# Seams of the expert layer: queries on half the tokens, finer waits, the last value blocks tile by tile

## The reference

```python
hp = layer_norm(ALPHA * hp + mix_p, ln1_g[l], ln1_b[l])
...
q = (tok @ w_q).astype(jnp.float32).reshape(n, PEER_HEADS, 2, PEER_DKEY // 2)
s1 = jnp.einsum('nhk,ek->nhe', q[:, :, 0], sk[0])
s2 = jnp.einsum('nhk,ek->nhe', q[:, :, 1], sk[1])
v1, i1 = lax.top_k(s1, PEER_TOPK)
v2, i2 = lax.top_k(s2, PEER_TOPK)
...
gate = jax.nn.softmax(top_s, axis=-1).astype(h.dtype)
...
act = jax.nn.gelu(jnp.einsum('nd,nhkd->nhk', t, u_tab[e]), approximate=False)
return jnp.einsum('nhk,nhkd->nd', g * act, v_tab[e])
...
hp = layer_norm(ALPHA * hp + peer_ffn(hp, *pw), ln2_g[l], ln2_b[l])
```

## Time and profile before

| | us |
|---|---|
| median of 3 runs | 2153.55 (2152.06 to 2166.17) |
| the profiled execution, its own time | 2161.72 |
| its span, first to last instruction | 2159.3 |
| TensorE busy | 2044.9 (95%) |
| VectorE busy | 1485.2 (69%) |
| moved by DMA | 682.97 MB, mean 316 GB/s |

### The profile page before, as it was taken

One profiled execution on the slowest core, in us unless ns is written; L12 is line 12 of the kernel. 1 busy time (PEld: TensorE's weight loads), 2 busy tenths in 40 slices (PEclk: granted clock), 3 DMA queues, 4 the chain that ended last, 5 costly groups with the idle time before them and its releaser, 6 DMA issues.

```text
span 2159.3 us, 33707 instructions
## 1 busy us (share of the span) xinstructions
PE 2044.9 (95%) x12186; PEld 1709.8 (79%) x12186; DVE 1485.2 (69%) x3108; ACT 742.2 (34%) x1111; POOL 787.3 (36%) x485
## 2 busy tenths in 40 slices
PE   7999999998978997999999999999979999999996
PEld 7999985555542346989999999999978888778784
DVE  1375125664662333678888879999789888988888
ACT  2232113443440001224333355555433333333332
POOL 4343210000210003336898841221365564656440
PEclk9999998999988998999999999999999999999998
DMA  9999987883968668936999977888999999999992
GB/s 325 346 315 311 318 324 292 341 354 139 339 235 318 235 221 323 347 116 223 352 361 357 340 284 274 306 299 302 359 388 390 389 393 393 389 385 391 387 387 104
DMA packets 202346, 682.97 MB, mean 316 GB/s; under 512 B 18305, under 2 KB 84225, under 8 KB 194177
## 3 DMA queue, kind: packets, MB, share of 16 engines
q1 hardware_dynamic: 150832, 439.29, 56.4%
q0 software_dynamic: 46080, 167.79, 20.3%
q10 hardware_dynamic: 5328, 74.52, 9.9%
HBM read 618.78 MB, written 196.32 MB: 377 GB/s over the span
## 4 chain that ended last, share of the span: by engine, by line
PE 58%; DMA 19%; DVE 9%; issue 9%; POOL 3%; ACT 2%; SPq 0%; POOLq 0%; DVEq 0%; ACTq 0%
DMA overlay<-peer_v 15%; PE bank L188 12%; PE bank L189 12%; PE bank L190 12%; PE bank L1426 5%; PE bank L2014 4%; POOL overlay L358 3%; DVE overlay L2212 3%; DVE arena L2027 2%; PE bank L644 2%; PE bank L628 2%; DMA arena<-cache_v 1%; ACT overlay L2131 1%; PE bank L694 1%; PE bank L667 1%
## 5 line engine op out<-in xcount | busy, mean ns | idle before, releaser
L188 PE MATMUL bank<-overlay 128*128 128x384 f32 (+4 forms) x2832 | 959.7, 339 | 46.5 <-DVE overlay L2216 17.0
L189 PE MATMUL bank<-overlay 128*128 128x384 f32 (+4 forms) x2832 | 946.2, 334 | 0.0
L190 PE MATMUL bank<-overlay 128*128 128x384 f32 (+4 forms) x2832 | 945.2, 334 | 0.0
L188 PEld LDWEIGHTS bank<-overlay 128*128 128x128 f32 (+1 forms) x2832 | 535.4, 189 | 87.0 <-issue 39.1
L189 PEld LDWEIGHTS bank<-overlay 128*128 128x128 f32 (+1 forms) x2832 | 535.3, 189 | 30.3
L190 PEld LDWEIGHTS bank<-overlay 128*128 128x128 f32 (+1 forms) x2832 | 534.5, 189 | 31.2
L1850 POOL DMA_INDIRECT arena<-peer_v,arena x160 | 267.4, 1671 | 228.0 <-DVE arena L2027 205.1
L1578 POOL TENSOR_TENSOR overlay<-overlay 128x1024 fp32r<-128x1024 f32 x86 | 206.5, 2404 | 316.0 <-ACT overlay L1571 312.9
L2027 DVE SCALAR_TENSOR_TENSOR arena<-arena 128x1024 f32<-128x1024 f32 x160 | 204.3, 1277 | 0.1
L1850 POOL DMA_INDIRECT arena<-peer_rows,arena x80 | 106.6, 1332 | 245.8 <-DVE arena L2022 225.0
L1571 ACT CAST overlay<-overlay 128x1024 fp32r<-128x1024 f32 x144 | 150.0, 1044 | 114.7 <-DMA overlay<-peer_u 90.6
(11 more groups left out here) (235 smaller groups left out, 2160.9 us busy)
## 6 DMA issues: line engine op xcount, KB each, us to landing
overlay<-peer_u SPq DMA_DIRECT2D x128, 512.0 KB, 7.6
overlay<-peer_v SPq DMA_DIRECT2D x128, 512.0 KB, 11.3
o_ks<-cache_k ACTq DMA_DIRECT2D x11, 4088.0 KB, 18.4
o_vsall<-cache_vall SPq DMA_DIRECT2D x21, 2044.0 KB, 23.5
arena<-cache_kT SPq DMA_DIRECT2D x32, 896.0 KB, 11.2
arena<-cache_v SPq DMA_DIRECT2D x56, 512.0 KB, 6.9
arena<-w_out SPq DMA_DIRECT2D x48, 512.0 KB, 5.6
act<-arena SPq DMA_DIRECT2D x128, 192.0 KB, 8.2
```

The lines of the kernel that those rows point to most:

```text
L188: pe.matmul(out, lhs[0], rhs[0], start=start, stop=False)
L189: pe.matmul(out, lhs[0], rhs[1], start=False, stop=False)
L190: return pe.matmul(out, lhs[1], rhs[0], start=False, stop=stop)
```

## The change

1. **Queries.** The first half of features 0 and 1 (24 matmuls each) is issued around the last `turn_h`: TensorE waits only for the splits of the first three tiles. ScalarE casts the first weights before and behind the last norm's root, GpSimd makes the first low part before that norm's end and the others behind it. The three DMAs L1541 move behind the queries.
2. **Up.** The copy into banks 4 and 5 moves behind the fourth Gelu; TensorE no longer waits for VectorE's copies of the scores.
3. **Value stage, start.** SyncE waits for two stores of each slot before the first group and for all behind it; ScalarE doesn't wait for the stores; VectorE waits for one slot's stores at each of blocks 2 to 5. One accumulator is cleared before the waits, the other behind block 0.
4. **Value stage, end.** Late rows are spread over 120 blocks; the norms of tile 3 and the sample tokens stand behind blocks 121 and 123; gain and bias of the norm are fetched ahead of the last group; the last four blocks are multiplied tile by tile, and each tile's norm waits for its own.

```diff
@@ pe_out
+            pe.wait_ge(h_lo, 2 * 3)
+            query_half(pe, 0, 0)
             turn_h(pe, 4)
+            query_half(pe, 1, 0)
@@ act_out
+                if i == 3:
+                    act.wait_ge(mixed, TILES)
+                    hi_of(act, 0, 0)
+                    hi_of(act, 1, 0)
                 act_root(act, n, i)
+                if i == 3:
+                    hi_of(act, 2, 0)
+                    hi_of(act, 3, 0)
...
-            for g in range(1, FOLD):
-                act.dma_start(h1[g * NS:(g + 1) * NS, QT], h1[0:NS, QT]).then_inc(h_folded, 16)
@@ pool_query
+            lo(0, 0)
+            pool.wait_ge(ln_step.sem, lnm["out", QT])
+            for s in range(1, 4):
+                lo(s, s)
@@ pe_query
+        def query_half(pe, f, half):
+            pe.wait_ge(u_lo, f + 1)
+            for c in range(DC):
+                mm = product(pe, bank[:, 2 * (f % 2) + half, 0:HALF], [w[:, f % 4, c] for w in us],
+                             [h[:, c, half * HALF:(half + 1) * HALF] for h in hh], c == 0, c == DC - 1)
+            return mm
...
+            def query(f):
+                if f >= 2:
+                    pe.wait_ge(q_kept, f + 1)
+                    query_half(pe, f, 0)
+                query_half(pe, f, 1).then_inc(q_ready, 1)
@@ act_query
-            act.wait_ge(mixed, TILES)
-            for s in range(4):
-                hi_of(act, s, 0)
...
+            for g in range(1, FOLD):
+                act.dma_start(h1[g * NS:(g + 1) * NS, QT], h1[0:NS, QT]).then_inc(h_folded, 16)
@@ act_up
-            act.wait_ge(s_ready, QF + 2)
-            act.wait_ge(s_kept, 2 * QF + 4)
-            act.copy(bank[:, 4:6, :], h1[:, DT].rearrange("p (b n) -> p b n", b=2)).then_inc(h_copied, 1)
...
+                if n == 3:
+                    act.wait_ge(s_kept, 2 * QF + 4)
+                    act.copy(bank[:, 4:6, :], h1[:, DT].rearrange("p (b n) -> p b n", b=2)).then_inc(h_copied, 1)
@@ pe_up
-            pe.wait_ge(s_kept, 2 * QF + 4)
@@ values
-        ROWS_END, FINAL_AT = PK - 4, (PK - 3, PK - 1)
+        ROWS_END, FINAL_AT, BY_TILE = PK - 8, (PK - 7, PK - 5), 4
@@ sp_values
-                sp.wait_ge(a_stored[s], 16 * (GROUPS + 1))
+                sp.wait_ge(a_stored[s], 16 * (1 + 2))
...
             group(0, 1)
-            with sp.Fori(1, PAIRS) as x:
+            for s in range(4):
+                sp.wait_ge(a_stored[s], 16 * (GROUPS + 1))
+            with sp.Fori(1, PAIRS - 1) as x:
...
+            group(PAIRS - 1, 0)
+            sp_norm2(sp)
+            group(PAIRS - 1, 1)
@@ act_values
-            for s in range(4):
-                act.wait_ge(a_stored[s], 16 * (GROUPS + 1))
...
-                    if last and j == 6:
-                        act_root(act, TILES, LAST[0])
+                    if last and j in (2, 4):
+                        act_root(act, TILES + j // 2 - 1, LAST[j // 2 - 1])
@@ pe_values
+                for j in range(8 - BY_TILE if last else 8):
+                    ready(j)
...
+                if last:
+                    for i in range(DT):
+                        for j in range(8 - BY_TILE, 8):
+                            if i == 0:
+                                ready(j)
+                            mm = tile(j, i)
+                        mm.then_inc(tile_done, 1)
@@ dve_values
+            dve.memset(acc3, 0.0).then_inc(acc_zeroed, 1)
             dve.wait_ge(u_done, PK)
             dve.wait_ge(g_done, SLABS * GS + 2)
-            for s in range(4):
-                dve.wait_ge(a_stored[s], 16 * (GROUPS + 1))
-            dve.memset(acc3, 0.0).then_inc(acc_zeroed, 1)
-            dve.memset(accS, 0.0).then_inc(acc_zeroed, 1)
...
+                if 2 <= a < 6:
+                    dve.wait_ge(a_stored[a - 2], 16 * (GROUPS + 1))
                 dve.tensor_tensor(ga[1][:, j], prod[j % 2], ga[0][:, j].bitcast(F32), ALU.subtract).then_inc(ga_lo, 1)
+                if a == 0:
+                    dve.memset(accS, 0.0).then_inc(acc_zeroed, 1)
@@ final_norm
-                    dve.wait_ge(vp_done, PK + 8)
+                    dve.wait_ge(tile_done, i + 1)
```

More of the change, by code:

```diff
@@ L1578, in lo @@
                 pool.tensor_tensor(us[1][:, s], uraw[s], us[0][:, s].bitcast(F32), ALU.subtract).then_inc(u_lo, 1)
-            with pool.Fori(0, (QF + ROWS_FROM) // 4) as x:
+            lo(0, 0)
+            pool.wait_ge(ln_step.sem, lnm["out", QT])
+            for s in range(1, 4):
+                lo(s, s)
+            with pool.Fori(1, (QF + ROWS_FROM) // 4) as x:
                 for s in range(4):
@@ L1604, in pe_query @@
             pe.sem_inc(s_ready, 2)
-            def query(f, s):
-                pe.wait_ge(u_lo, f + 1)
-                pe.wait_ge(q_kept, f + 1)
-                for half in range(2):
-                    for c in range(DC):
-                        mm = product(pe, bank[:, 2 * (s % 2) + half, 0:HALF], [w[:, s, c] for w in us],
-                                     [h[:, c, half * HALF:(half + 1) * HALF] for h in hh], c == 0, c == DC - 1)
-                mm.then_inc(q_ready, 1)
+            def query(f):
[3 more added lines that the diff above has]
+                query_half(pe, f, 1).then_inc(q_ready, 1)
             def score(f, s):
@@ L1625, in pe_query @@
                     if s < 4:
-                        query(k * 4 + s, s)
+                        query(k * 4 + s)
                     if s:
@@ L2152, in pair, with ready, tile @@
             def pair(x, first=False, last=False):
-                for j in range(8):
+                def ready(j):
                     pe.wait_ge(ga_lo, x * 8 + (j + 3))
                     pe.wait_ge(v_lo, x * 8 + (j + 5))
+                def tile(j, i):
+                    for half in range(2):
+                        mm = product(pe, bank[:, 2 * i + half, :], [w[:, j, i * P:(i + 1) * P] for w in ga],
+                                     [v[:, j, half * 512:(half + 1) * 512] for v in vs], first and j == 0, last and j == 7)
+                    return mm
+                for j in range(8 - BY_TILE if last else 8):
+                    ready(j)
                     for i in range(DT):
-                        for half in range(2):
-                            mm = product(pe, bank[:, 2 * i + half, :], [w[:, j, i * P:(i + 1) * P] for w in ga],
-                                         [v[:, j, half * 512:(half + 1) * 512] for v in vs], first and j == 0, last and j == 7)
+                        mm = tile(j, i)
                     mm.then_inc(vp_done, 1)
-                    if last and j == 4:
+                    if last and j == 1:
                         unfold(pe)
+                if last:
[3 more added lines that the diff above has]
+                                ready(j)
+                            mm = tile(j, i)
+                        mm.then_inc(tile_done, 1)
             pair(0, first=True)
@@ L2235, in sp_final @@
             sp.dma_start(lnb2, t["ln2_b"]).then_inc(ln2_in, 16)
+        def sp_final(sp):
             for n, i in enumerate(LAST):
@@ L2276, in act_final @@
         def act_final(act):
-            for n in range(1, TILES):
+            for n in range(2, TILES):
                 act_root(act, TILES + n, LAST[n])
```

4 lines of the change are left out of this document (2 added, 2 removed).

## The result

| | before | changed |
|---|---|---|
| median, first comparison (us) | 2157.64 (4 runs) | 2132.55 (4 runs) |
| ratio, with its 95% interval | | 0.989 (0.9862 to 0.9918) |
| median, second comparison (us) | 2155.47 (15 runs) | 2137.3 (10 runs) |
| ratio, with its 95% interval | | 0.993 (0.9907 to 0.9953) |
| profiled execution | 2161.72 | 2126.72 |

The change makes the kernel 25.1 us faster in the first comparison and 18.2 in the second. Forecast were 2131.5 us and a gain of 21.9.

The account below looks back on a forecast made before the run. TensorE was taken to bound the kernel upstream, TensorE and the DMA within 3% in the value stage; -11.2-6.1-4.6 = -21.9 from the 2153.55 median gave 2131.5 us (own range 2126 to 2137, full range 2118 to 2145).

Parts of the forecast that it names:

- rival B: Tail and pace: packed rows cost their full 7.5 us and an upstream gain is smaller; -15.0, 2138.5 us; chance 0.23.
- Part 1, forecast -11.2: Queries: first half features start around the last norm, second query's copy at 838.3, not 849.6; bounds 9.3 to 11.2.
- it fell near 826, and a restart at 824.7 comes before that: Queries: TensorE restarts before its granted clock falls, so no slow clock; otherwise it costs about 1.9 us.
- a first query at half clock: Queries: sign that the prediction is wrong, the first query running at TensorE's slow clock.
- Covered by 4 us: Queries: the fifth query's weights are ready at 849.4, and TensorE asks for them at about 853.
- Part 2, forecast -6.1: Before the up stage: wait shrinks by 4.3 us and the slow start, costed at 1.8, vanishes; bounds 5.2 to 7.1.
- the issues begin with the start of the operation before them and take 2.81: Before the up stage: three DMA issues on ScalarE's queue delay its signals to 957.3, leaving TensorE about 1 us idle.
- Part 3, forecast -0.7: Value stage start: TensorE starts 7.3 us earlier, but the DMA limit returns all but 0.7 as waits; bounds 0 and 7.3.
- Rival A: Value stage: supply is not the limit, so the 7.3 us arrive and the tail gives more; -33.6, 2120 us; chance 0.22.
- Part 4, forecast -3.9: Value stage end: packed rows cost 2.5 us, last matmul ends 6.4 later, but one norm follows instead of three.
- VectorE's two norms now stand ahead of four splits: Value stage end: the reason given for TensorE's last matmul ending 6.4 us later than before, at 2146.2.
- Rival C: From the queries on: DMA engines are the limit, upstream gains return as waits; +4.4, 2158 us; chance 0.05.

Follow-up runs that it names:

- the single parts: The kernel before with the lines of one part of the change each, four kernels; ratios 0.9968, 0.9962, 1.0001 and 1.0006.
- in the pair: One profile of the kernel before against one of the changed kernel; profiled executions 2161.72 and 2126.72 us.
- part 2 alone: The kernel before with only the copy into banks 4 and 5 moved behind the fourth Gelu; 2149.16 us, ratio 0.9962.
- in company: The changed kernel with waits and clearings at the head of the value stage as before; 2137.32 us against 2137.3, ratio 0.9916.
- fewer bytes: The kernel before with gates of eight of twelve slabs unread, plus the finer waits at the value stage's start; executed once, 2132.87 us.
- The kernel with the late norm: The changed kernel with the sample tokens' norm behind block 127, not 123; 2135.52 us, ratio 0.9905 to the kernel before.
- fewer gates: The kernel before with the gates of eight of the twelve slabs left unread in the value stage; executed once, 2156.57 us.

## Why the prediction was right

The time (2131.5, measured 2132.55 and 2137.3), the gain (21.9, measured 25.1 and 18.2; by stretches 22.8 and 19.8) and the mechanism held. Part of the near hit is luck: against the single parts (10.1, 8.1, 0.9 and 2.2, together 21.3) two terms were 1.1 and 1.7 too large and one 2.0 too small. The second comparison's 2137.3 lies 0.3 above the forecast's own range and 1.2 below rival B's time, so the time alone doesn't choose between them; the terms do. Term by term:

**Part 1, forecast -11.2, measured -10.1.** The first query matmul came 3.72 us behind tile 3 (forecast about 3.7) and the copy 18.5 behind it. The prediction's last paragraph gives 28.5 for that copy, which is the length before; its own working says 838.3-821.1 = 17.2. What failed is one step: "it fell near 826, and a restart at 824.7 comes before that". That read a time of falling out of one seam. Here the clock fell with the restart, after 3.72 us of idleness (in three of the seven profiles ahead of it, in four behind), and the first 15 matmuls took 0.225 us each from start to start ((816.45-813.08)/15), not 0.126, which is 1.5 us; the text's lower bound, 9.3, had costed 1.9. The rule of the Trainium skill ("TensorE: Matmul & The Clock Gate", What's actually happening), by which the clock comes back only after sustained work, fits the windows of 813 to 816, and "a first query at half clock", named as a sign of rival B, came true. B's second half, rows at their full 7.5 us, did not: they cost 3.6. "Covered by 4 us" was too sure as well: in two of seven profiles 3.2 and 3.6 us went back to late weights.

**Part 2, forecast -6.1, measured -7.2 in the pair, -8.1 alone.** The upper bound (7.1, "if they blocked nothing") was the true one. The step that failed is "the issues begin with the start of the operation before them and take 2.81": they began 0.4 us ahead of the last cast and took 0.62+1.44 = 2.1, so they were over 0.4 us before TensorE ended its last score and not 0.8 behind it. With part 2 alone no issue stands there, and the wait is gone just the same. The selections of VectorE cost nothing, as costed.

**Part 3, forecast -0.7, measured -0.9 alone, 0 to -3 in company.** The step that decided the case held: a seam of 7.2 us was taken away and the stage took it back. With fewer bytes the same edit gave 8.5, so it is the supply that took it back; that the supply's limit is the DMA rate and not the latency of its loop rests on the estimate above (401 GB/s needed, 391 moved). Rival A (2120, "the supply is not the limit") falls with it.

**Part 4, forecast -3.9, measured -2.2 alone.** The size was near, the reason only half right. Packing the rows delayed block 120's split by 3.6 us (forecast 2.5) and its first matmul by 7.1. The last matmul came 40.1 behind the split, forecast 39.7; but by my text because "VectorE's two norms now stand ahead of four splits", and by the runs because TensorE is 3.5 us behind the split when block 120 comes (with no rows left VectorE makes the last splits faster than TensorE multiplies: at blocks 118 to 120 TensorE is 1.9, 2.7 and 3.5 us behind them) and then works through 34.9 us of its own and 1.7 that the second norm costs. The kernel with the late norm showed that: 7.3 us sooner on VectorE made this stretch 1.7 shorter, not the 5.3 by which the forecast's 39.7 exceeds TensorE's own 34.4. Block 127 came 27.5 us behind block 120, as forecast, by luck: gain and bias, which had 2 us in that sum, were no term: issued at 2071.48, waited for by nobody at 2078.14. The wait that did stand there, 1.90 us for the unfolding, I hadn't seen; it filled their place. The last paragraph's "last matmul 10 us, not 17, before VectorE's last operation" is a slip too: the sum has one norm there, 5.5, and 5.7 was measured.

**Rival C** (the queries at the DMA limit too) lives only in those 3 us of late weights; part 2 kept its 8.1 us to the end. The prediction let C hold by the 358 GB/s of the Trainium skill ("DMA: Bandwidth & Descriptors", Where 436 GB/s comes from). That doesn't follow: the up stage before moved 313 GB/s on average and 292 to 298 in 1200 to 1500, which is below the figure. And the 387 to 389 GB/s of the value stage contradict it again.

What stays open: why TensorE's clock stands at 1.2 GHz for 55 us upstream of tile 3 in one execution and for 85 in another, and the 3.3 us of wander of "120 ready", which bounds what can be said of parts 3 and 4 apart.

## What to carry to other kernels

Before you cost a wait at its length, look whether the engine behind it is held by its supply later in the stage. A high DMA share is a reason to look, not the answer: it was 1.04 where the earlier start gave 0.9 us, and 1.00 with fewer gates, where it gave 8.5. What told the two apart were the casts' waits for DMA (133.8 and 17.5 us) and the rate that the consumer would need beside the rate that was moved. Where the supply is the limit, an earlier start only moves the wait, and the bytes themselves are the place to gain. The end of a kernel is different, since work taken from behind the last matmul counts whole, less what it costs to make room for it. And compare stretches between events of the kernel, with the same kernel profiled twice, before you trust a difference of 3 us.

## What the runs showed of the hardware

- TensorE's clock after a short idle time: in the changed kernel the granted clock stood at 1.00 through 3.72 us of idleness and read 0.63 and then 0.50 from the restart on, until 816.5, some 3.4 us. In four of the seven profiles with this wait the clock fell when the engine was already working again, in three shortly before. In the seam before it stood idle for 5.73 us and had fallen before the restart. So this wait cost its length and 1.5 us more.
- One kernel's time and TensorE's clock: the changed kernel's four executions took 2126.55 and 2126.72 us at a mean granted clock of 0.982 and 0.983, and 2138.38 and 2140.52 at 0.978 and 0.977. Over 14 profiles the end of tile 3 came 0.44 us later for each us that the clock stood at 1.2 GHz ahead of it.
- DMA issues on ScalarE's queue begin while a copy of ScalarE is still running, ahead of a cast that precedes them in the list. Between 932.33 and 934.43 three of them held up only what came behind them: the load of the Gelu's table at 934.73 shows 0.99 us of idle time put down to issue, with 3.2 us to spare before the first Gelu.
- The stage's traffic: 387 to 389 GB/s over 500 us at share 1.04 to 1.05, in both kernels, and 380 GB/s at 1.00 with fewer gates. It isn't one fixed ceiling in GB/s: the changed kernel moved 409 at share 1.04 in 1500 to 1560, at the end of the up stage, and the one with fewer gates 403 at 1.03 in 1700 to 1800.
